# The four weight slots of a one-core fp32r kernel, placed off the multiples of 256 bytes in SBUF

## The chip, the cores and the metric

One core of one Trainium2 chip. The metric is the time of one execution on the device, in microseconds. The profile shows one execution, instruction by instruction.

## What is computed

Two layers, one behind the other, on x of 1024 positions by 1024 features in float32. The first is a hybrid of a gated causal convolution and a sliding window attention, the second a forgetting attention followed by a convolutional FFN and a gated embedding:

```python
def hybrid_layer(x, ...):
    u = rms_norm(x, norm_g) @ w_in                     # split in nine parts
    y_c = b_c * causal_depthwise_conv(c_c * v_c, conv_w) * silu(z_c)
    y_a = y_c @ w_conv_out
    o = sliding_window_attention(rms_norm(q), rms_norm(k), v, sinks) * silu(z_a)
    merged = g_a * y_a + g_b * (o @ w_attn_out)        # g: sigmoid gates
    return x + merged @ w_out

def second_block(x, p, ...):
    x = layer_norm(ALPHA * x + fox_mixer(x, ...))      # 16 heads, causal, cumulative forget bias
    u, g = split(x @ w_up)                             # 2 x 2816 columns
    x = layer_norm(ALPHA * x + (gelu(causal_dwconv(g)) * u) @ w_down)
    return x + sigmoid(x @ w_gate + b_gate) * (p @ w_proj)
```

## The kernel before

Activations lie feature-major: a tensor of 1024 features is `[128, KT=8, 1024]`, and a matmul has 128 x 128 weights as its stationary operand and 128 x 512 activations as its moving operand. For precision each float32 operand is held as a sum of two float32r tensors, a high part and a low part (`a_hi`, `a_lo`, `b_hi`, `b_lo` for activations, `whi`, `wlo` for weights), and a product is three matmuls: whi x hi, whi x lo, wlo x hi.

Weights come in units of 128 output columns, `[128, 8, 128]`. SyncE loads the two halves of a unit into `raw[0]` and `raw[1]`. GpSimd (`split`, lines 639 and 641) rounds a half into `whi[slot]` and writes the rest into `wlo[slot]`. TensorE then reads eight slices of 512 bytes of the slot (`product`, line 804; `part`, line 867, where the matmuls of a unit are mixed with those of the attention). A unit's slot is its number modulo 2, so that one is filled while the other is read. These are `whi0`, `whi1`, `wlo0` and `wlo1`, each 4096 bytes a partition.

Other places use the same four slots by halves. In the paired projections (twenty of the convolution's and the gates' weight pairs, eighteen of the FFN's) each pair is made as seven block products instead of eight (`pairs_of`, line 1124); their weights go through a ring of seven half slots, of which four are halves of `whi0`, `whi1` and their low parts (`conv_ring`, `up_ring`) and three lie elsewhere (`cr` tiles, or the upper halves of `b_hi` and `b_lo`). There ScalarE writes the high part (line 1687) and GpSimd the sums (line 644) and the low part (line 654). The down product (`down_product`, line 1291) takes its weights from the four slots by halves as well, with ScalarE writing whi (line 2172) and GpSimd wlo (line 765). The last product (line 1311) takes them from the four slots in part. Slots 2 to 5 (`whi2` and so on) are laid over `a_lo`, are not among the four, and are used only for a part of the attention output (`OUT_SLOTS`, ten of sixteen halves of 24 matmuls) and for two of the first FFN tiles (`FFN_SLOTS`, four half passes of 24).

All engines run their own programs, with semaphores between them. The order of TensorE's work is written out by hand.

The placement in SBUF is by hand too. `base` is the first free byte of the partition, rounded up to 32; it is 16512 here, 128 past a multiple of 256. `fixed` puts a tile at `base + top[0]` and moves `top[0]` on by its size, rounded up to 32. The order is: four small tiles of 32 bytes, `raw0` and `raw1` of 2048 each, the four slots, then `ident`, the masks, the constants, `a_hi`, `a_lo`, `b_hi`, `b_lo` (32 KiB each), and from `over_at` on an area in which each stage lays its own tiles (`overlay`). `a_hi_at` and `over_at` are multiples of 256, so the halves and blocks that matmuls read start at multiples of 256 as well. In the area of the pairs `up_g` has 4104 bytes, and `up_u` and `a22_1` behind it lie 32 bytes past a multiple of 256; `xv` and `a22_0` lie at one.

Of the kernel before, what the change touches and what calls it, by code (L numbers as in the profile page):

```python
# [18 lines left out]
F32R = mybir.dt.float32r  # L19
# [4 lines left out]
P = 128  # L24
D = 1024
S = 1024
KT = D // P
# [184 lines left out]
def build(nc, xT, weights, pair_weights, down_weights, cols, pT, out, y_scr, ga_scr, x_scr, ple_scr, t_scr, g_scr, c_scr, h_scr,  # L212
          wd_scr, xs_scr):
    ctx = ExitStack()
    with ctx:

        top = [0]
        base = -(-nc.sbuf_base // 32) * 32

        def fixed(name, shape, dt):  # L220
            n = int(np.prod(shape[1:])) * 4
            t = nc.alloc_sbuf_tensor_at(name, [P, *shape[1:]], dt, offset=base + top[0])
            top[0] += -(-n // 32) * 32
            return t
# [5 lines left out]
        row_sum = fixed("row_sum", [P, 8], F32)  # L230
        sink_exp = fixed("sink_exp", [P, 8], F32)
        raw = [fixed(f"raw{b}", [P, HALF], F32) for b in range(2)]
        whi = [fixed(f"whi{s}", [P, KT, P], F32R) for s in range(2)]
        wlo = [fixed(f"wlo{s}", [P, KT, P], F32R) for s in range(2)]
        ident = fixed("ident", [P, P], F32)
        ident_r = fixed("ident_r", [P, P], F32R)
        mask_r = fixed("mask_r", [P, 3 * P], F32R)
# [2986 lines left out]
```

## Time and profile before

| | us |
|---|---|
| median of 2 runs | 2476.61 (2476.07 to 2477.16) |
| the profiled execution | 2476.72 |
| its span, first to last instruction | 2475.0 |
| TensorE busy with matmuls | 2440.3 |
| VectorE busy | 1550.9 |
| GpSimd busy | 1323.5 |
| ScalarE busy | 1088.5 |

The profile names engines PE (TensorE matmul), PEld (TensorE weight load), DVE (VectorE), ACT (ScalarE), POOL (GpSimd) and SP (SyncE). Matmuls are pipelined: a matmul's own duration in the trace is longer than the distance from its start to that of the next, and it is the distance that adds up. In names such as `bank<-a_hi,whi` the first is what is written, then the moving operand, then the stationary one; numbers of buffers are left out, so `whi` can be any of six slots.

### The profile page before, as it was taken

The numbers are of one execution on the slowest core, as the hardware profiler recorded it, in microseconds if no ns is written. First come the engines' busy times: TensorE is split into PE (matmuls) and PEld (weight loads), VectorE is DVE, ScalarE is ACT, GpSimd is POOL, SyncE is SP. The second block draws the span as 40 slices with busy tenths as digits, with TensorE's granted clock in tenths as the row PEclk, the third lists the DMA queues.
The fourth block names the chain that finished last, engine by engine and source line by source line (L and its number), as shares of the span: only waits on it lengthen the run. The fifth ranks groups of instructions, "written<-read, shape, count | busy, mean of one in ns | idle before, by whom it ended". The sixth has DMA issues, their size and how long they took to land. (4 is left out here: it accounts for less than half of the span.)

```text
span 2475.0 us, 36098 instructions
## 1 busy us (share of the span) xinstructions
PE 2440.3 (99%) x11658; PEld 2013.9 (81%) x11658; DVE 1550.9 (63%) x2240; ACT 1088.5 (44%) x2010; POOL 1323.5 (53%) x1092
## 2 busy tenths in 40 slices
PE   8999999999999999999999999999999999999999
PEld 5888888888788878888888888877788888878877
DVE  6555552344777785435666666756678777777785
ACT  4332333301666661126777777832433333344441
POOL 3798887433455554432111111244279888666683
PEclk9999999999999999999999999999999999999999
DMA  3222223579210015321111111431133333387652
GB/s 112 90 75 67 70 68 113 180 267 331 77 34 25 26 35 187 132 99 60 43 43 43 43 43 43 138 109 52 47 111 115 123 119 110 140 281 217 190 182 80
DMA packets 126498, 267.24 MB, mean 108 GB/s; under 512 B 13872, under 2 KB 14000, under 8 KB 126400
## 3 DMA queue, kind: packets, MB, share of 16 engines
q1 hardware_dynamic: 84800, 157.85, 20.2%
q10 hardware_dynamic: 41600, 108.19, 12.2%
q8 instruction: 49, 0.80, 0.1%
q14 instruction: 49, 0.40, 0.1%
HBM read 198.02 MB, written 67.96 MB: 107 GB/s over the span
## 5 line engine op out<-in xcount | busy, mean ns | idle before, releaser
L639 POOL TENSOR_SCALAR whi<-raw 128x512 fp32r<-128x512 f32 x194 | 142.1, 732 | 783.9 <-PE bank L867 394.4
L641 POOL TENSOR_TENSOR wlo<-raw,whi 128x512 fp32r<-128x512 f32 x194 | 275.2, 1419 | 16.2
L804 PE MATMUL bank<-a_hi,whi 128*128 128x512 f32 x464 | 182.6, 394 | 1.5 <-issue 1.5
L804 PE MATMUL bank<-b_lo,whi 128*128 128x512 f32 x464 | 181.4, 391 | 0.0
L654 POOL TENSOR_TENSOR wlo<-a,whi 128x512 fp32r<-128x512 f32 x114 | 165.3, 1450 | 17.1 <-ACT whi L1687 16.9
L867 PE MATMUL bank<-b_hi,whi 128*128 128x512 f32 x384 | 156.4, 407 | 0.0
L867 PE MATMUL bank<-b_hi,wlo 128*128 128x512 f32 x384 | 150.7, 392 | 0.0
L867 PE MATMUL bank<-b_lo,whi 128*128 128x512 f32 x384 | 149.9, 390 | 0.0
L804 PE MATMUL bank<-b_hi,whi 128*128 128x512 f32 x336 | 131.7, 392 | 0.7 <-DVE b_lo L2300 0.4
L804 PE MATMUL bank<-a_hi,wlo 128*128 128x512 f32 x336 | 130.8, 389 | 0.0
L804 PE MATMUL bank<-a_lo,whi 128*128 128x512 f32 x336 | 130.8, 389 | 0.0
L1687 ACT ACTIVATE whi<-a 128x512 fp32r<-128x512 f32 x114 | 70.7, 627 | 132.4 <-PE bank L1124 54.9
L1566 ACT ACTIVATE fp<-fp,row_inv 128x128 f32<-128x128 f32 (+7 forms) x128 | 99.4, 777 | 24.3 <-DVE row_inv L2508 23.8
L2499 DVE CUSTOM_DVE_ANT_0 fp<-score,fc 128x128 f32<-128x128 f32 (+7 forms) x128 | 96.8, 756 | 20.5 <-PE flip L1047 9.0
L1560 ACT ACTIVATE fp<-fp,neg_max 128x128 f32<-128x128 f32 (+7 forms) x128 | 99.1, 775 | 20.6 <-DVE neg_max L2503 18.7
L804 PEld LDWEIGHTS bank<-a_hi,whi 128*128 128x128 f32 x464 | 87.1, 188 | 22.1 <-issue 3.7
L804 PEld LDWEIGHTS bank<-b_lo,whi 128*128 128x128 f32 x464 | 87.1, 188 | 18.5 <-issue 0.7
L867 PE MATMUL bank<-a_hi,whi 128*128 128x512 f32 x240 | 100.1, 417 | 0.5 <-DVE s_z L2388 0.5
L867 PE MATMUL bank<-a_hi,wlo 128*128 128x512 f32 x240 | 94.0, 392 | 0.0
L867 PE MATMUL bank<-a_lo,whi 128*128 128x512 f32 x240 | 93.8, 391 | 0.0
L804 PE MATMUL bank<-b_hi,wlo 128*128 128x512 f32 x240 | 93.4, 389 | 0.0
L804 PE MATMUL bank<-b_lo,wlo 128*128 128x512 f32 x224 | 87.2, 389 | 0.0
(710 smaller groups left out, 7618.6 us busy)
## 6 DMA issues: line engine op xcount, KB each, us to landing
raw<-in_w SPq DMA_DIRECT2D x206, 256.0 KB, 2.6
a<-in_pairs SPq DMA_DIRECT2D x152, 256.0 KB, 2.7
wd_scr<-wd SPq DMA_DIRECT2D x55, 256.0 KB, 5.0
wd<-in_down SPq DMA_DIRECT2D x44, 256.0 KB, 4.7
xs_scr<-made ACTq DMA_DIRECT2D x40, 256.0 KB, 2.6
fc<-c_scr ACTq DMA_DIRECT2D x16, 512.0 KB, 3.6
h_scr<-up_y ACTq DMA_DIRECT2D x13, 512.0 KB, 2.6
raw<-wd_scr SPq DMA_DIRECT2D x26, 256.0 KB, 2.8
```

Of the source, the lines that this page charges most:

```text
L639: nc.gpsimd.tensor_scalar(hi, src, 1.0, 1.0, ALU.mult, ALU.mult).then_inc(w_hi, 1)
L641: nc.gpsimd.tensor_tensor(lo, src, hi.bitcast(F32), ALU.subtract).then_inc(w_lo, 1)
L654: nc.gpsimd.tensor_tensor(ring[1][pos], src[:].rearrange("p (k c) -> p k c", c=P), ring[0][pos].bitcast(F32), ALU.subtract).then_inc(ww_lo, 1)
L804: last = nc.tensor.matmul(psum_ap, ws[w][:, k, :], a[:, kt, hs(h)], start=(first and i == 0 and j == 0), stop=(final and i == n - 1 and j ...
L867: last = nc.tensor.matmul(bank[b][:], ws[slot][:, k, :], a[:, k, hs(h)], start=(k == 0 and j == 0), stop=(k == KT - 1 and j == 2))
L1560: nc.scalar.activation(fp[s % 3][:, 0:w], fp[s % 3][:, 0:w], ACT.Exp, bias=neg_max[:, one], accum_out=row_sum[:, one]).then_inc(fx.exp, 1)
L1566: nc.scalar.activation(fp[s % 3][:, 0:w], fp[s % 3][:, 0:w], ACT.Copy, scale=row_inv[:, s % 4:s % 4 + 1]).then_inc(fx.prob, 1)
L1687: nc.scalar.activation(ring[0][pos], src[:].rearrange("p (k c) -> p k c", c=P), ACT.Copy).then_inc(ww_hi, 1)
L2499: v.tensor_tensor_reduce(out=fp[s % 3][:, 0:w], in0=score[s % 2][:, 0:w], in1=fc[hh][:, 0:w], scale=SCALE, scalar=-3.0e38, op0=ALU.subtrac ...
```

## The change

The four slots get a place of their own each, counted from a multiple of 256 bytes: whi0 at 64, whi1 at 32, wlo0 at 192 and wlo1 at 160 past. Behind them the place is moved on to the next multiple of 256, and all other tiles follow in the same order. Nothing else is touched.

```diff
@@ -230,8 +230,13 @@
         row_sum = fixed("row_sum", [P, 8], F32)
         sink_exp = fixed("sink_exp", [P, 8], F32)
         raw = [fixed(f"raw{b}", [P, HALF], F32) for b in range(2)]
-        whi = [fixed(f"whi{s}", [P, KT, P], F32R) for s in range(2)]
-        wlo = [fixed(f"wlo{s}", [P, KT, P], F32R) for s in range(2)]
+        def slot(name, past):
+            top[0] += (past - base - top[0]) % 256
+            return fixed(name, [P, KT, P], F32R)
+
+        whi = [slot("whi0", 64), slot("whi1", 32)]
+        wlo = [slot("wlo0", 192), slot("wlo1", 160)]
+        top[0] += (-base - top[0]) % 256
         ident = fixed("ident", [P, P], F32)
         ident_r = fixed("ident_r", [P, P], F32R)
         mask_r = fixed("mask_r", [P, 3 * P], F32R)
```

## Rows read from the trace of the kernel before

**Rows 1.** The page: busy time by engine, and the granted clock in 40 slices
```profile
PE 2440.3 (99%) x11658; PEld 2013.9 (81%) x11658; DVE 1550.9 (63%) x2240; ACT 1088.5 (44%) x2010; POOL 1323.5 (53%) x1092
...
PEclk9999999999999999999999999999999999999999
```

**Rows 2.** The waits of TensorE: us in total, times, longest
```profile
PE score L824 <- ACT sq L1337: 7.1, 2, 6.0
PE pv L938 <- POOL sp_lo L703: 5.2, 9, 1.2
```

**Rows 3.** The chain of waits, a piece of the down product: start, us, what
```profile
2175.45 7.48 PE flip L1291 x33
```

**Rows 4.** Busy time by stretch: length, PE, PEld, DVE, ACT, POOL, clock, DMA, GB/s
```profile
950.00:1100.00 150.00, 150.00 (x663) 124.21 (x662) 67.70 (x68) 17.76 (x28) 63.51 (x55) 1.00 0.40 133
```

**Rows 5.** The timeline in a pair's products: start us, us, engine, line
```profile
299.81 0.39 PE L1124 MATMUL bank<-ct4lo,cr1hi 128*128 128x512 f32 x1
299.82 0.19 PEld L1124 LDWEIGHTS bank<-ct4hi,cr1lo 128*128 128x128 f32 x1
300.04 0.39 PE L1124 MATMUL bank<-ct4hi,cr1lo 128*128 128x512 f32 x1
...
301.40 0.39 PE L1124 MATMUL flip<-a_hi,cr2lo 128*128 128x512 f32 x1
```

**Rows 6.** The whole span, instructions with tile whi (PE, PEld, ACT, POOL), then wlo (PE, PEld, POOL)
```profile
0.00:2475.00 2475.00, 1551.51 (x4968) 918.34 (x4968) 142.65 (x229) 766.30 (x633) 1.00 0.33 108
...
0.00:2475.00 2475.00, 968.82 (x2484) 466.23 (x2484) 619.60 (x431) 1.00 0.33 108
```

**Rows 7.** Busy time by stretch, columns as in rows 4
```profile
500.00:550.00 50.00, 50.00 (x222) 41.42 (x221) 22.38 (x28) 0.00 (x0) 18.99 (x17) 1.00 0.80 271
...
1900.00:1950.00 50.00, 50.00 (x222) 41.44 (x221) 38.72 (x40) 15.90 (x25) 46.25 (x30) 1.00 0.34 115
...
1900.00:2150.00 250.00, 250.00 (x1105) 207.07 (x1104) 191.55 (x192) 79.34 (x120) 218.34 (x144) 1.00 0.34 115
```

**Rows 8.** Line 1124, weight loads: duration ns min/median/max
```profile
L1124 PEld LDWEIGHTS bank<-a_hi,whi x160: 186/188/188, 94.1 to 460.5; 128*128 128x128 f32 x160
...
L1124 PEld LDWEIGHTS bank<-b_hi,wlo x144: 187/188/188, 1820.9 to 2150.4; 128*128 128x128 f32 x144
```

**Rows 9.** The timeline in the sliding window attention at 760 us
```profile
759.73 0.39 PE L867 MATMUL bank<-a_lo,whi 128*128 128x512 f32 x1
...
759.97 0.40 PE L867 MATMUL bank<-a_hi,wlo 128*128 128x512 f32 x1
...
760.66 0.39 PE L867 MATMUL bank<-a_hi,wlo 128*128 128x512 f32 x1
```

**Rows 10.** The timeline in the sliding window attention at 906 us
```profile
905.94 0.39 PE L867 MATMUL bank<-a_lo,whi 128*128 128x512 f32 x1
...
906.86 0.40 PE L867 MATMUL bank<-a_hi,wlo 128*128 128x512 f32 x1
```

**Rows 11.** Lines 2585 and 1692 by tile: duration ns min/median/max
```profile
L2585 DVE TENSOR_TENSOR up_u<-up_u,flip x36: 674/682/689, 1831.7 to 2167.4; 128x512 f32<-128x512 f32 x36
...
L2585 DVE TENSOR_TENSOR xv<-xv,flip x20: 686/689/690, 103.8 to 456.2; 128x512 f32<-128x512 f32 x20
...
L1692 ACT ACTIVATE up_u<-bank x18: 597/599/602, 1831.0 to 2154.8; 128x512 f32<-128x512 f32 x18
L1692 ACT ACTIVATE xv<-bank x10: 578/598/599, 103.1 to 443.2; 128x512 f32<-128x512 f32 x10
```

**Rows 12.** Lines 654 and 641, GpSimd's low parts: duration ns min/median/max
```profile
L654 POOL TENSOR_TENSOR wlo<-a,whi x114: 1282/1296/2288, 84.4 to 2140.7; 128x512 fp32r<-128x512 f32 x114
...
L654 POOL TENSOR_TENSOR cr0lo<-raw,cr0hi x20: 1285/1297/1312, 99.1 to 451.5; 128x512 fp32r<-128x512 f32 x20
L654 POOL TENSOR_TENSOR cr1lo<-a,cr1hi x20: 1287/1292/2293, 100.3 to 454.2; 128x512 fp32r<-128x512 f32 x20
...
L641 POOL TENSOR_TENSOR wlo<-raw,whi x194: 1263/1297/2260, 10.7 to 1801.9; 128x512 fp32r<-128x512 f32 x194
```

## The prediction

> **What bounds the kernel now.** I read the page's busy table first [rows 1]: TensorE is busy 2440.3 of 2475.0 us, 99%, and nothing else is near it (VectorE 63%, GpSimd 53%, ScalarE 44%). The slices under it show the same in every stretch, with the granted clock at the top throughout (printed 9 in the page, 1.00 in the stretch table), so all of it is at 2.4 GHz. The waits of TensorE [rows 2] are small: the largest line is 7.1 us in two waits, the second 5.2 us over nine. So what the kernel costs is how many matmuls it issues times the distance from one to the next. A change of addresses leaves the number alone, and can only act on the distance, or slow another engine until TensorE waits for it.
>
> The distance comes from three places that agree. In the chain of waits the down product has pieces of 33 matmuls in 7.48 us [rows 3], 226.7 ns each. In the stretch from 950 to 1100 us, 663 matmuls touch 150 us [rows 4]; two of them lie over an edge, so 150/661.8 is 226.7 ns. The timeline at 299.8 us [rows 5] has seven steps in 1.59 us, 227 ns. In cycles of 2.4 GHz that is 544 for 512 columns: 32 cycles or 13.3 ns more than one column a cycle (213.3 ns). That this surplus exists at all is the one thing in the trace at which a placement could aim.
>
> **How much work reads the four slots.** The stretch view restricted to the weight tiles gives 4968 matmuls with whi and 2484 with wlo, 7452 of 11658 [rows 6]. Names there leave the slot number out, so those of slots 2 to 5 come off. They are used by ten of the sixteen halves of the attention output (`OUT_SLOTS`, 10 x 24 matmuls) and four half passes of the first FFN tiles (`FFN_SLOTS`, 4 x 24), together 336. 7116 matmuls read a slot that moves: 7116 x 0.2267 = 1613 us of the time hangs on them. Of the two reads of a matmul only the stationary one changes place; the moving one (a_hi, b_hi and the like) keeps its place relative to 256.
>
> **What the change moves.** By the allocator, `base` plus the four small tiles and both raw buffers ends at a multiple of 256, and each slot is 4096 bytes, so before, all four start at 0 past 256. After, whi0 is 64 past, whi1 32, wlo0 192, wlo1 160, with gaps of 64, 224, 160 and 224 bytes, and 96 more before `ident`: 768 bytes in all. 768 is three times 256, so every later tile keeps its residue. No instruction, wait, DMA or buffer is added or taken away, no queue is passed, and no DMA writes or reads the four slots (raw, from which they are filled, stays where it was). Instruction terms: 0.
>
> **Term 1: TensorE's pace.** No row of before has a stationary operand off a multiple of 256, so the price must be bounded.
> From the neighbouring evidence first. With DMA at 0.80 of its engines, GpSimd 18.99 and ScalarE 0.00 of 50 us the stretch from 500 us begins 222 matmuls; with GpSimd at 46.25, VectorE at 38.72 and ScalarE at 15.90 the stretch from 1900 us begins 222 as well [rows 7]. TensorE's pace does not see what else goes on in SBUF, although everything there starts at the same residue. Nor does the tile matter: within one unit the steps over k are 512 bytes apart and all take 227 ns, and the weight load takes 188 ns at median wherever it is [rows 8]. It begins with the matmul before it and is over some 30 ns ahead of the next start (0.01 + 0.19 of 0.23 us in print) [rows 5]. So a load that is a little longer, as by one extra line at its ends, is hidden: an estimate, 1/8 more of 188 ns is 23.5 ns, still inside that. I take 0 as the likeliest value for term 1.
> Lower bound: the surplus is a clash of the stationary read with the moving read, both at 0 past 256, and the new residues remove it. Then -13.3 ns x 7116 = -94.9 us.
> Upper bound: after attention work, when the two streams have not yet fallen into step, 512-column matmuls stand further apart: from 759.73 to 760.66 four steps in 0.93 us, 232 ns each, the longest 0.24 in print [rows 9], and from 905.94 to 906.86 four steps in 0.92 us, 230 ns [rows 10]. If the new residues kept them so, it is +3.3 ns x 7116 = +23 us by the last of these, and by the longest single step, taken as 236 ns, +9.3 ns x 7116 = +66 us.
>
> The Trainium skill, TensorE: Matmul & The Clock Gate, section Back-to-back issue gap, gives N/2.4 + 2.5 ns for the gap, 215.8 ns for 512 columns; this trace has 226.7 [rows 3]. The same page, under Step-by-step, says that the stationary and the moving operand have separate SBUF read ports, so that loading the next weights takes nothing from the running matmul. By the second rule the placement is worth nothing; if instead the 10.9 ns between the first rule and the trace were such a clash, an estimate is 7116 x 10.9 = 77.6 us gained. No run here shows which.
>
> **Term 2: the engines that fill the slots.** GpSimd writes wlo, GpSimd or ScalarE write whi. `up_u` and `a22_1` already lie 32 past a multiple of 256, behind the 4104 bytes of `up_g`. VectorE's sum into up_u takes 682 ns at median, the same line into xv, which starts at 0 past, 689. ScalarE's copy into up_u takes 599 ns, into xv 598 [rows 11]. GpSimd's `cr1lo<-a,cr1hi` reads a22_0 and a22_1 in turn and has its median, 1292 ns, 5 ns over its minimum, beside 1297 for cr0lo, which reads no such tile [rows 12]. So 32 bytes past costs these engines nothing. GpSimd's write is the one that isn't shown. It has some room: from 1900 to 2150 us GpSimd is busy 218.3 of 250 us [rows 7], 16.6 us of each pair's 19.04 (84 matmuls x 0.2267), 2.4 us free for the four slot operations of a pair. Term 2: 0.
>
> Sum: 0 + 0. The profiled execution took 2476.72 us around its span of 2475.0, and the median is 2476.61, so nothing is to be converted: 2476.6 us.
>
> **The rivals.**
> *The clash goes away.* For: the surplus is there, it's the same for all 512-column matmuls, and the paces after attention show that something between the two streams depends on their phase. Against: the surplus stays 13.3 ns over all k, all tiles and beside any traffic. Time: 2476.6 - 94.9 = 2381.7 us; if only one of the two slot pairs gets out of the way, half of it, 2429 us.
> *The reads fall out of step.* This ends on the other side: a weight read that starts 32 or 64 past a boundary meets the moving stream, which starts on one, at a worse phase, and each such matmul takes the 236 ns of the longest step after attention [rows 9] instead of 226.7. Place: every unit from the slots, most plainly in L804 and L1291, where nothing hides a longer distance since TensorE is the bound. Price: 9.3 x 7116 = 66 us, 2543 us. It passes 2% (49.5 us) from 7.0 ns a matmul on. Against: a start off the boundary can as well be better.
> *GpSimd becomes the bound.* If its operations on a slot take 2.3 us instead of 1.3, as its longest ones do (2288 ns) [rows 12], a pair has 4 x 1.0 = 4.0 us more against 2.4 free, 1.6 us in each of 38 pairs: +61 us, 2537 us. It begins at +0.6 us (46%) an operation. Against: that nothing in the other operands of this kind shows a price for 32 bytes [rows 11, 12].
> *The change is something else than it says:* every tile from `ident` on moves by 768 bytes, which changes the residue to 512, and both operands with it. Stretches that read no slot (the `fp`/`fv` matmuls of L1062) would then change too. Their step over blocks is 512 bytes, though, so I give it 0.03 and a time within 1% of before.
>
> **How the numbers follow.** No change beyond a few microseconds: 0.62. Clash gone: 0.15, of which two thirds pass 2%. Out of step: 0.15, of which a little over half is small enough to stay within 2%. GpSimd: 0.05. Everything shifted: 0.03. Within 2%, about what a measurement of this kernel can tell from no change: 0.62 + 0.05 + 0.08 + 0.03 = 0.78; faster by over 2% 0.10; slower by over 2% 0.12. The forecast's own range is 2470 to 2484. The 8 in 10 range takes in half of the clash (2429) and the whole of the out-of-step case (2543), which leaves out the full clash and a GpSimd far over its room.
>
> **What would show it.** Right: matmuls with whi and wlo at 227 ns from start to start, 33 in 7.48 us at the down product, 222 in 50 us, weight loads at 188 ns, POOL's `wlo<-raw,whi` median near its 1297 ns of before [rows 12]. Wrong by rival one: about 234 matmuls begin in 50 us, and those of L1124 that read cr or ct tiles as stationary stay at 227 while those from whi drop. Wrong by rival two: 212 to 218 in 50 us with the same contrast inside L1124, and perhaps a different pace per slot, which would say which of the four residues hurts. Wrong by rival three: TensorE waits for POOL at L654 or L641 and the pace inside a run stays 227.

## The result, and the profile after

| | before | after |
|---|---|---|
| median of 2 runs, us | 2476.61 | 2504.2 (2503.95 to 2504.46) |
| profiled execution's span, us | 2475.0 | 2502.7 |
| matmuls begun from 950 to 1100 us | 663 | 650 |

The changed kernel takes 1.0112 times the time of the one before, 95% interval 1.0096 to 1.0128: 27.6 us longer, outside the forecast's own range (2470 to 2484) and inside the 8 in 10 range (2429 to 2543). The instruction counts are the same. Lines after the edit are five higher: L1124 is now L1129, L1291 L1296, L804 L809.

The page after, busy time by engine, beside [rows 1]:

```profile
PE 2469.7 (99%) x11658; PEld 2013.2 (80%) x11658; DVE 1546.8 (62%) x2240; ACT 1089.3 (44%) x2010; POOL 1327.5 (53%) x1092
```

TensorE alone is longer, by 29 us; the weight loads and the other engines are within 5 us of before. Its waits, beside [rows 2] (us in total, times, longest), have not grown:

```profile
PE score L829 <- ACT sq L1342: 7.2, 2, 6.2
PE pv L943 <- POOL sp_lo L708: 4.8, 9, 1.2
```

So the time must lie in the distance from matmul to matmul. Two pieces of the chain of waits in the down product, beside [rows 3], and the stretch of [rows 4]:

```profile
2198.67 7.68 PE flip L1296 x33
2206.34 7.66 PE pv L1296 x33
```

```profile
950.00:1100.00 150.00, 150.00 (x650) 121.51 (x649) 68.46 (x70) 18.31 (x29) 63.83 (x55) 1.00 0.41 140
```

33 matmuls take 7.67 us instead of 7.48: 232.4 ns each instead of 226.7, at the same granted clock. The durations say whether the weight loads have grown. Line 1129 (min/median/max ns), weight load and matmul; before, all three matmuls have a median of 389 ns:

```profile
L1129 PEld LDWEIGHTS bank<-a_hi,whi x160: 186/188/189, 95.3 to 467.1; 128*128 128x128 f32 x160
L1129 PE MATMUL bank<-a_hi,whi x160: 392/394/473, 95.3 to 467.3; 128*128 128x512 f32 x160
...
L1129 PE MATMUL bank<-a_lo,whi x160: 388/392/396, 95.6 to 467.6; 128*128 128x512 f32 x160
...
L1129 PE MATMUL bank<-a_hi,wlo x160: 391/398/398, 95.8 to 467.8; 128*128 128x512 f32 x160
```

The load of the moved tile still takes 188 ns; the matmul's record grew, by 3 to 9 ns. The ends of matmuls are modelled in the profile, so this shows that the load is no longer than before, but not which of the two reads holds up the other. I summed the distances between starts by product, leaving out those of 245 ns or more (a wait is in them):

```
512-column matmuls             before ns   after ns   more, us
L804, slot that moved             226.87     231.75     10.9
L867, slot (mixed with attention) 229.61     232.15      4.3
L1124, slot                       226.70     231.67      9.0
L1124, other stationary tile      226.73     227.51      1.0
L1291, slot                       226.82     232.04      4.8
L1311, slot (the us: with others) 227.27     231.95      0.8
```

That is 31 us; 3 to 4 us come back in the distances of 245 ns and more and between smaller matmuls, which leaves the 27.7 of the span. Matmuls whose stationary tile did not move are nearly untouched: the 1 us of those in L1124 lies in the first nine or so after a slot and in the last one before the next, and L804's matmuls on the slots laid over `a_lo` have 227.1 ns before and after. GpSimd's operation on a slot, for which a rival had a price, has medians of 1301 and 1296 ns after (before 1296 and 1304):

```profile
L659 POOL TENSOR_TENSOR wlo<-a,whi x114: 1286/1301/3592, 85.3 to 2163.7; 128x512 fp32r<-128x512 f32 x114
L659 POOL TENSOR_TENSOR wlo<-raw,whi x38: 1285/1296/1769, 96.4 to 2160.2; 128x512 fp32r<-128x512 f32 x38
```

### The profile page after: what moved, and what is told of

It is laid out like the page before. It is cut to its first block and busy times, and to the rows that moved or that the text cites. A ratio compares the mean times of both kernels' runs of the same rounds, so it can differ in the third digit from the quotient of the medians.

```text
span 2502.7 us, 36098 instructions
## 1 busy us (share of the span) xinstructions
PE 2469.7 (99%) x11658; PEld 2013.2 (80%) x11658; DVE 1546.8 (62%) x2240; ACT 1089.3 (44%) x2010; POOL 1327.5 (53%) x1092
## 5 line engine op out<-in xcount | busy, mean ns | idle before, releaser
L809 PE MATMUL bank<-a_hi,whi 128*128 128x512 f32 x464 | 184.8, 398 | 2.1 <-issue 1.5
L809 PE MATMUL bank<-b_lo,whi 128*128 128x512 f32 x464 | 182.9, 394 | 0.0
L809 PE MATMUL bank<-b_hi,whi 128*128 128x512 f32 x336 | 133.2, 396 | 0.5 <-DVE b_lo L2305 0.4
L809 PE MATMUL bank<-a_hi,wlo 128*128 128x512 f32 x336 | 132.3, 394 | 0.0
L809 PE MATMUL bank<-a_lo,whi 128*128 128x512 f32 x336 | 132.0, 393 | 0.0
L809 PEld LDWEIGHTS bank<-a_hi,whi 128*128 128x128 f32 x464 | 87.2, 188 | 25.0 <-issue 3.7
L809 PEld LDWEIGHTS bank<-b_lo,whi 128*128 128x128 f32 x464 | 87.1, 188 | 20.0 <-issue 0.7
L809 PE MATMUL bank<-b_hi,wlo 128*128 128x512 f32 x240 | 94.3, 393 | 0.0
L809 PE MATMUL bank<-b_lo,wlo 128*128 128x512 f32 x224 | 87.9, 392 | 0.0
```

The costliest lines, as they stand in the source:

```text
L809: last = nc.tensor.matmul(psum_ap, ws[w][:, k, :], a[:, kt, hs(h)], start=(first and i == 0 and j == 0), stop=(final and i == n - 1 and j ...
```

## The experiments

Theory R: the pace is set by the difference between the place of the stationary and that of the moving operand, modulo 256. Rivals: A, the stationary operand's own place; J, a change of place from one stationary operand to the next; and that moving everything else by 768 bytes did it. All edits are to the changed kernel unless said otherwise, and `...` marks lines left out. Each ratio is to the kernel before, measured beside it, with its 95% interval.

### The shift of everything else alone

```diff
-        whi = [slot("whi0", 64), slot("whi1", 32)]
-        wlo = [slot("wlo0", 192), slot("wlo1", 160)]
-        top[0] += (-base - top[0]) % 256
+        whi = [slot("whi0", 0), slot("whi1", 0)]
+        wlo = [slot("wlo0", 0), slot("wlo1", 0)]
+        top[0] += 768
```

> The four slots stay at 0 past a multiple of 256, only everything behind them moves by the change's 768 bytes. Theory (the slots' residues cost the time): as before, 2476 to 2478 us, 227 ns from matmul to matmul. Rival (the shift of all other tiles by 768, which changes their residue to 512, costs it): near 2504 us.

2476.1 us, ratio 1.0001 (0.999 to 1.0013). In the stretches from 300 (pairs) and from 975 us (plain units) 443 matmuls touch 100 us each, as in the kernel before:

```profile
300.00:400.00 100.00, 100.00 (x443) 82.84 (x442) 46.76 (x49) 31.75 (x48) 82.26 (x58) 1.00 0.25 78
975.00:1075.00 100.00, 100.00 (x443) 82.84 (x442) 41.85 (x43) 12.02 (x19) 41.77 (x36) 1.00 0.41 141
```

The rival is out. The difference between stationary and moving operand, a multiple of 512 before, was 256 past one here: a step of 256 costs nothing.

### Everything by 32 bytes, from the kernel before

```diff
-        base = -(-nc.sbuf_base // 32) * 32
+        base = -(-nc.sbuf_base // 32) * 32 + 32
```

> All tiles, slots and everything else, 32 bytes further on, so that stationary and moving operands keep the same residue and both are off a multiple of 256. Theory R (it is the difference between the stationary and the moving operand's residue that counts): 2476 to 2478 us. Rival A (it is the stationary operand's own residue, a read that crosses one more boundary): slower, 2495 to 2510 us. Rival J (a change of residue from one stationary operand to the next): 2476 to 2478 us.

2477.2 us, ratio 1.0003 (0.9992 to 1.0015); mean distance in plain units 226.7 ns:

```profile
975.00:1075.00 100.00, 100.00 (x443) 82.84 (x442) 42.15 (x44) 12.03 (x19) 41.79 (x36) 1.00 0.41 142
```

All slots are off the multiples of 256 and nothing is lost. Rival A is out.

### One residue for all four, and one for each slot

```diff
-        whi = [slot("whi0", 64), slot("whi1", 32)]
-        wlo = [slot("wlo0", 192), slot("wlo1", 160)]
+        whi = [slot("whi0", 64), slot("whi1", 64)]
+        wlo = [slot("wlo0", 64), slot("wlo1", 64)]
```

> All four slots at 64 past. Theory R and rival A: slower, 2490 to 2510 us, with a pace of 229 to 235 ns in every matmul that reads a slot. Rival J (only a change of residue between successive stationary operands costs): 227 ns inside the units, 2476 to 2480 us.

2511.3 us, ratio 1.0141 (1.0112 to 1.0171), more than the change and just over the 2490 to 2510 that I gave. The stretch from 975 us has 430 matmuls instead of 443:

```profile
975.00:1075.00 100.00, 100.00 (x430) 80.60 (x429) 46.28 (x46) 12.02 (x19) 41.79 (x36) 1.00 0.39 132
```

Within a unit nothing changes residue here, so J is out as the cause: no such change is needed for the cost. The distances alternate between 231 and 236 ns, mean 233.3.

The next three have the two parts of a slot at one residue, and another one in the other slot, so that one run shows two (`slot("whi0", 128), slot("whi1", 96)` and the same for wlo, and so on):

> whi0 and wlo0 at 128 past, whi1 and wlo1 at 96. Rival J: 227 ns inside every unit, about 2478 us. Theory R and rival A: a pace of its own for each slot, so units alternate in pace; at 128 and 96 it may lie on either side of 227 ns, which nothing so far says; if a placement can remove the surplus at all it should show at one of the residues tried.

2511.2 us, ratio 1.0141 (1.0111 to 1.017).

> whi0 and wlo0 at 224 past, whi1 and wlo1 at 192. Theory R: a steady pattern for each slot, means of 229 to 234 ns, 2495 to 2515 us. If some residue were better than 0, a slot here would be under 226.7 ns.

2499.9 us, ratio 1.0094 (1.0065 to 1.0123).

> whi0 and wlo0 at 32 past, whi1 and wlo1 at 160. Theory R: as the run before, 229 to 234 ns and 2495 to 2515 us. With it, all multiples of 32 modulo 256 have been tried with the two parts of a slot at one residue.

2512.5 us, ratio 1.0145 (1.0115 to 1.0174).

### The slots at 0, everything else at 64

```diff
-        whi = [slot("whi0", 64), slot("whi1", 32)]
-        wlo = [slot("wlo0", 192), slot("wlo1", 160)]
-        top[0] += (-base - top[0]) % 256
+        whi = [slot("whi0", 0), slot("whi1", 0)]
+        wlo = [slot("wlo0", 0), slot("wlo1", 0)]
+        top[0] += (64 - base - top[0]) % 256
```

> The four slots at 0 past a multiple of 256 as in the kernel before, and everything behind them, the moving operands among it, at 64 past. Theory R (the difference between stationary and moving operand, modulo 256, sets the pace): the 7116 matmuls that read a slot are slow, 231 to 234 ns, though no slot has moved, and the mean pace is that of a slot at 192 past with moving operands at 0 (slot 1 of the run s0_224_s1_192); matmuls with cr, ct, b_hi or b_lo as the stationary operand, which moved together with the moving ones, stay at 227; total 2500 to 2515 us. Rival A (the stationary operand's own residue): the reverse, slots 227 and the others slow, under 2490 us.

2487.1 us, ratio 1.0049 (1.003 to 1.0069). The total that I gave (2500 to 2515) and the 231 to 234 ns were wrong; the link that theory R asked for holds. The steady distances repeat 226, 229, 232 ns, mean 228.9, and slot 1 of the run with 192 repeats 226, 229, 232 ns, mean 228.9. The matmuls of the pair products with an unmoved difference stay at 226.7. Slots that never moved became slow since the moving operand did: theory R.

```profile
975.00:1075.00 100.00, 100.00 (x439) 82.05 (x438) 45.10 (x46) 12.66 (x20) 43.31 (x37) 1.00 0.39 134
```

The down product's pieces in the chain of waits are between the other two levels, 7.55 us for 33, where all64 has 7.70:

```profile
2205.79 7.55 PE pv L1296 x33
2213.34 7.55 PE flip L1296 x33
```

```profile
2212.65 7.70 PE pv L1296 x33
2220.35 7.70 PE flip L1296 x33
```

### The high parts at 0, the low parts at 128

```diff
-        whi = [slot("whi0", 64), slot("whi1", 32)]
-        wlo = [slot("wlo0", 192), slot("wlo1", 160)]
+        whi = [slot("whi0", 0), slot("whi1", 0)]
+        wlo = [slot("wlo0", 128), slot("wlo1", 128)]
```

> Both whi at 0 past, both wlo at 128. Theory R: the extra time sits in the matmul during which the next stationary operand is read from 128, so that in a triple only the second (low part times whi, while wlo is loaded) is longer, the other two stay near 227; mean 228 to 230, total 2485 to 2500 us. If it instead goes with the operand that the matmul itself multiplies by, the third (times wlo) is the longer one. Rival J alone (a change of residue) is out already if all64 was slow with none.

2497.7 us, ratio 1.0085 (1.0056 to 1.0114). In a triple the first matmul takes 226.7 ns, the second, beside which wlo is loaded, 232.5, and the third, which multiplies by wlo, 234.2; mean 231.1, over the 228 to 230 that I gave. Each of my two forms named only one of the two long ones. Nor do the paces of two residues add up: two matmuls at the 226.7 ns of 0 and one at the 232.6 of 128 (table below) would have a mean of 228.7. So although J isn't the cause, the order in which places follow one another counts too.

### Steps under 32 bytes

`fixed` places tiles at multiples of 32, so the slots became views of one tile. This edit is to the kernel before, and those of the next section go on from it:

```diff
-        whi = [fixed(f"whi{s}", [P, KT, P], F32R) for s in range(2)]
-        wlo = [fixed(f"wlo{s}", [P, KT, P], F32R) for s in range(2)]
+        slots = fixed("wslots", [P, 4 * KT * P + 192], F32R)
...
+        def slot(at):
+            return slots[:, at // 4:at // 4 + KT * P].rearrange("p (k c) -> p k c", c=P)
+        places, at = [], 0
+        for past in (16, 240, 16, 240):
+            at += (past - at) % 256
+            places.append(at)
+            at += 4096
...
+        whi = [slot(places[0]), slot(places[1])]
+        wlo = [slot(places[2]), slot(places[3])]
+        top[0] += (-base - top[0]) % 256
```

> The slots as views of one tile, so that steps under 32 bytes can be had: whi0 and wlo0 at 16 past, whi1 and wlo1 at 240. Theory R (pace set by the difference to the moving operand modulo 256): if the cost changes gradually with the difference, both slots lie between 226.7 and 233.3 ns; if any difference costs, 229 to 234 ns. A version faster than both kernels needs a residue under 226.7 ns; this is one of four last candidates. Total 2485 to 2515 us.

2485.3 us, ratio 1.0034 (1.0022 to 1.0045).

> whi0 and wlo0 at 4 bytes past (one element), whi1 and wlo1 at 8. Theory R with a phase of whole elements: already one element of difference changes the steady pattern away from 226, 227, 227. If instead the difference counts in blocks (of 16 or 32 bytes), both slots stay at 226.7 ns and the total near 2476 us. A start off 16 bytes could also cost the load itself, which would show as weight loads longer than 188 ns.

2497.1 us, ratio 1.0082 (1.0053 to 1.0111). One element of difference is enough: the difference doesn't count in blocks. The median weight load stays 188 ns at 4 and 8 past.

One thing came out faster here. GpSimd's subtraction into a slot has a median of 1094 ns, against 1297 before [rows 12]; it stays at 1292 to 1305 in the changed kernel and in the three runs at 16 or 240 past. It is worth nothing in this kernel, where TensorE is the bound, but GpSimd's busy time falls from 1323.5 to 1229.7 us:

```profile
L654 POOL TENSOR_TENSOR wslots<-raw,wslots x178: 1087/1094/2055, 10.5 to 1816.0; 128x512 fp32r<-128x512 f32 x178
```

All the residues together. Means over 252 distances between matmuls in plain units (about 945 to 1090 us), both parts of a slot at the given difference; taking more or fewer matmuls at the edges of a unit moves them by up to 0.3 ns:

```
difference, bytes      0      4      8     16     32     64     96    128    160    192    224    240
plain units, ns    226.7  232.4  230.6  233.3  233.3  233.3  234.4  232.6  233.3  228.9  233.3  228.3
```

No difference is below 226.7. The changed kernel, with 64/192 and 32/160, has 231.9 and 231.4. Its slot with 32/160 doesn't even have one pace: the unit from 959 to 970 us runs at 233.3 ns, the later ones at 231.1.

### Why 16 and 240 past cost nothing in the pair products

In that run the same slots, and so the same differences, gave 226.9 ns in L1124's matmuls, but 233.3 and 228.3 in the plain units. Theory H: a small difference leaves two steady states, and what ran before selects one; the pair products follow matmuls with difference 0. Rival N: the neighbour slot with its other residue disturbs the plain units.

```diff
-        for past in (16, 240, 16, 240):
+        for past in (16, 16, 16, 16):
```

> All four slots at 16 past. In s0_16_s1_240 the same two differences gave 226.7 ns in the pair products and 233.3 (at 16) and 228.3 ns (at 240) in the plain units. Theory H (a small difference leaves two steady states, and what ran before selects between them; the pair products come in from tiles with difference 0 and stay in the good one): pair products again at 226.7 to 227 ns, plain units at 233.3 in both slots, total 2485 to 2495 us. Rival N (the neighbour slot with another residue did it): plain units fall back to 227 when all slots are alike, total 2476 to 2480 us.

2495.0 us, ratio 1.0074 (1.0057 to 1.009). Plain units 233.3 ns in both slots, pair products 226.8. The stretches from 300 (pairs) and 975 us (plain units) show both states in one kernel:

```profile
300.00:400.00 100.00, 100.00 (x443) 82.84 (x442) 47.37 (x50) 31.24 (x47) 83.71 (x58) 1.00 0.26 79
975.00:1075.00 100.00, 100.00 (x430) 81.01 (x429) 43.58 (x44) 12.02 (x19) 41.84 (x36) 1.00 0.39 132
```

> All four slots at 240 past. Theory H: pair products at 226.7 to 227 ns, plain units at about 228.3 in both slots, total 2479 to 2485 us. Rival N: plain units at 227, 2476 to 2478 us. If small differences on this side could beat 0, this run would be under 2476 us; I do not expect it.

2478.0 us, ratio 1.0004 (0.9995 to 1.0014): 228.3 ns in both slots of the plain units, 226.8 in the pair products. The total lies between the two forecasts (2476 to 2478, 2479 to 2485) and decides nothing; the distances do. Rival N is out. It remained that the kind of product might decide (rival K). So I disturbed the pair products: one more matmul of 128 columns ahead of each pair, once on the kernel with the slots at 16 and once on the kernel before, at 0.

```diff
                     pe.wait_ge(ww_lo, n * 7 + pos + 1)
+                    if pos == 0:
+                        nc.tensor.matmul(dst[:, 0:P], ring[0][0][:, 0, :], x_hi[:, 0, 0:P], start=True, stop=True)
                     for k in range(KH):
```

> The slots at 16 past, and one additional matmul of 128 columns ahead of each of the 38 pairs (its product is overwritten by the first one of the pair), to push the two read streams out of step where the pair products used to stay at 226.7 ns. Theory H (steady states selected by what ran before): the 48 matmuls of a pair that read a slot now run at 233 ns, the following ones from tiles with difference 0 fall back to 227; 38 x 48 x 6.7 ns = 12 us and 38 x 0.06 = 2 us for the added matmuls over all16, about 2509 us. Rival K (the kind of product decides): pair products stay at 227, and only the 2 us come on top, about 2497 us.

2508.3 us, ratio 1.013 (1.01 to 1.0159), 13.4 us over all16. The slot matmuls of the pairs went from 226.8 to 233.0 ns, the others are at 227.3. The distances of one pair: the slot matmuls repeat 235, 233, 233, 234, 231, 234; with the first tile of difference 0 they go 224, 231, 236, 228, 232, 231 and are at 226, 227, 227 again. The timeline around the added matmul, and the stretch from 300 us, 438 matmuls (five of them added) against 443:

```profile
309.58 0.39 PE L1139 MATMUL flip<-a_hi,cr2lo 128*128 128x512 f32 x1
309.81 0.22 PE L1133 MATMUL bank<-a_hi,wslots 128*128 128x128 f32 x1
309.86 0.45 PE L1139 MATMUL bank<-a_hi,wslots 128*128 128x512 f32 x1
310.15 0.40 PE L1139 MATMUL bank<-a_lo,wslots 128*128 128x512 f32 x1
```

```profile
300.00:400.00 100.00, 100.00 (x438) 81.76 (x437) 46.62 (x49) 30.73 (x46) 84.07 (x58) 1.00 0.25 76
```

> The kernel before with the same additional matmul ahead of each pair. By both theories the streams fall back to 227 ns within some ten matmuls, since the difference is 0: 2 us for the matmuls and up to 38 x 10 x 5 ns = 2 us for the way back, 2478 to 2481 us.

2481.1 us, ratio 1.0019 (1.0008 to 1.003). After the added matmul the distances are 231, 235, 229, 232, 230, 228 ns and from then on 226, 227, 227. The slot matmuls of the pairs have a mean of 227.2 ns. Theory H holds: the same disturbance dies out within a few matmuls at difference 0, and lasts for all the slot matmuls of the pair at 16. The last product (L1311) shows the same with nothing added: in all16 its 48 slot matmuls from 2444 us run at 233.3 ns and the 96 others at 226.7, and in all16_kick all 144 run at 226.7, though nothing was added in this product. The added matmul is a bit dearer than I gave (4.9 us in all), since the added matmul and the first one behind it together cost near 119 ns more than a matmul in step, where I had counted the 60 ns of the added one alone.

## Why the prediction was wrong

*What bounds the kernel.* Right: TensorE is the bound by its number of matmuls times their distance, and the change acts on nothing else. So was it that every matmul reading a slot is touched: in all64 none of those of L1124 and L1291 is left at 226 or 227 ns.

*Instruction terms, term 2 and rival three.* Right, and rival three is out: same instructions, GpSimd's and ScalarE's median durations on the slots within 8 ns of before, no new waits.

*Term 1, "I take 0 as the likeliest value".* This step failed; it measured +4.7 to +5.2 ns a moved matmul in the products that are not mixed with attention. Its evidence, that the 227 ns hold beside any traffic and for every k and tile, is true, but every one of those rows has a difference of 0 modulo 256 between stationary and moving operand. Rows that all share the condition which the edit removes can't say what it is worth. The weight load, on whose 30 ns of room I leaned, never grew: the distance between matmuls did all the same, and the sum had no term for that.

*The bounds.* The upper one came from the right rows. The distances after attention [rows 9, 10] are of the size that the changed kernel then keeps: 232 and 230 ns in those rows, 231.9 and 231.4 in its plain units. I had priced rival two by the longest single step, 236 ns, and put 66 us on it; by the mean of the four steps of [rows 9], 232.5 - 226.7 = 5.8 ns x 7116 = 41 us, and 27.6 is still less. Some 6 us of the rest are the matmuls of L867: they were out of step before already (229.6 ns, 41% of them at 226 or 227) and so had only 2.5 ns to lose. The others lost 4.7 to 5.2 ns instead of 5.8, some 5 us, and 3 to 4 us came back in waits and gaps.

*Rival one, the clash removed.* Wrong for all eleven differences tried beside 0: none brought the distance under 226.7 ns. What the 13.3 ns above one column a cycle are made of stays open. The Trainium skill, TensorE: Matmul & The Clock Gate, Step-by-step, says that the two operands have separate read ports and that a load takes nothing from the running matmul. No run here shows the ports. The second half isn't what the runs show in this kernel: rest64 changed only where the moving operand lies against the slots and put 2.2 ns on the distance; all64, which moved the slots, put 6.7 ns on it.

*Rival four.* Out by gap768.

*The chances.* Rival two, at 0.15, was the case that came, with the signs that were given for it: 650 matmuls in 150 us are 217 in 50, and inside L1124 the slot matmuls went to 231.7 ns and the others to 227.5. Its size was not foreseen: that 2504 us lies in the 8 in 10 range owes much to the range reaching to 2543. Between an unmeasured 0 and a mechanism that the trace showed at work after each attention step, 0.62 against 0.15 was too sure.

What is shown and what isn't: that the pace depends on the difference of the operands' places modulo 256, down to one element, and for 16 past on what ran before, is shown. The difference alone doesn't give the pace, as hi0_lo128 and the two paces at 16 show, and no rule here forecasts the number for a given difference. That it comes from the two reads meeting in the same part of SBUF at some phase fits, but it was only argued; no run took one of the two reads away. A kernel faster than the one before was not found: of all runs only shift32, gap768 and all240 are level with it.

## What to carry to other kernels

Where TensorE is the bound and works in float32r with a new weight load for each matmul, keep stationary and moving operands at the same place modulo 256 bytes, and look at the distance between starts (here 226.7 ns in step, 228 to 234 out of it), not at durations or busy shares, which stay at 99%. A place that costs nothing behind one kind of work can cost 3% behind another, so judge a placement in each product of the kernel. When an edit takes away a condition that all rows of the trace share, the rows are no evidence for its price, and the rows where the engine falls out of its rhythm are the better guide.

## What the runs showed of the hardware that I had not expected

- The pace of 512-column float32r matmuls has several steady patterns: one value at a difference of 0, 231 and 236 ns in turn at 64, six values at 16, nine in the changed kernel's slot with 64/192. Their means often come out even: 544, 548 and 560 cycles of 2.4 GHz (226.7, 228.3, 233.3 ns).
- It is the difference between the operands that counts, not the stationary one's place: 32 bytes on both, 1.0003; 64 bytes on the stationary one, 1.0141; 64 bytes on the moving one, 1.0049. The two directions aren't alike (64: 233.3 ns; 192, which is -64: 228.9; 16: 233.3; 240: 228.3).
- At 16 past the same addresses run at 226.8 or at 233 ns, by what ran before; a single matmul of 128 columns tips them over.
- Weight loads of 512 bytes that start at 4 or 8 bytes past a multiple of 256 take the same 188 ns at median, and GpSimd's subtraction into such a slot takes 1094 ns instead of 1297.
